# The FFN's gate and up projections made token-major, with an SBUF-to-SBUF step and block transposes

## What is computed

```python
h = rmsnorm_2(x, ffn_norm[l])
g = causal_dwconv(jnp.einsum('bsd,df->bsf', h, w_gate[l]), conv_w[l], conv_b[l])
u = jnp.einsum('bsd,df->bsf', h, w_up[l])
x = x + jnp.einsum('bsf,fd->bsd', jax.nn.silu(g) * u, w_down[l])
```

## Time and profile before

| | |
|---|---|
| median of 3 runs | 2015.3 us (2014.77 to 2015.37) |
| the profiled execution | 2015.61 us |
| its span, first to last instruction | 2013.7 us |
| mean granted TensorE clock | 0.999 |
| TensorE busy | 1996.9 us (99%) |
| VectorE busy | 1431.3 us (71%) |
| ScalarE busy | 1044.3 us (52%) |
| GpSimd busy | 404.8 us (20%) |
| DMA | 374.89 MB, 186 GB/s in the mean |

### The profile page before, as it was taken

How to read it: one execution, slowest core, us unless ns; L and a number is a source line. 1 busy time by engine, 2 the same in 40 slices (tenths; PEclk the granted TensorE clock), 3 DMA queues, 4 the chain that set the end, 5 groups by cost and what they waited for, 6 DMA issues and landing times.

```text
span 2013.7 us, 28421 instructions
## 1 busy us (share of the span) xinstructions
PE 1996.9 (99%) x11082; PEld 1734.2 (86%) x11082; DVE 1431.3 (71%) x2004; ACT 1044.3 (52%) x1575; POOL 404.8 (20%) x379
## 2 busy tenths in 40 slices
PE   8999999999999999999999999999999999999998
PEld 7888998888888888888888888888888888888886
DVE  6776788788788666876656679777775457777654
ACT  6654544466534654644555655455454345545444
POOL 0014544300000444430222335111010000101010
PEclk9999999999999999999999999999999999999999
DMA  9765666567655334665454446655666665656564
GB/s 331 232 190 149 194 186 198 188 212 242 221 171 171 120 121 133 191 203 196 154 170 147 147 163 189 203 187 182 188 195 191 197 189 189 191 187 197 190 195 150
DMA packets 103798, 374.89 MB, mean 186 GB/s; under 512 B 11728, under 2 KB 13168, under 8 KB 103152
## 3 DMA queue, kind: packets, MB, share of 16 engines
q1 hardware_dynamic: 103376, 372.54, 58.5%
q10 hardware_dynamic: 288, 0.52, 0.1%
HBM read 370.92 MB, written 2.10 MB: 185 GB/s over the span
## 4 chain that ended last, share of the span: by engine, by line
PE 95%; DVE 2%; DMA 2%; ACT 1%; issue 0%; SPq 0%; ACTq 0%
PE psg L574 42%; PE psg L575 22%; PE psg L641 3%; PE psg L643 2%; PE psg L642 2%; PE pst L669 2%; PE pss L669 2%; PE pst L671 2%; PE pss L670 2%; PE pst L670 2%; PE pss L671 2%; PE psg L615 1%; PE pst L615 1%; DMA s_stage<-in_mk 1%; DVE s_w L1827 1%; PE psg L618 1%
## 5 line engine op out<-in xcount | busy, mean ns | idle before, releaser
L1827 DVE TENSOR_TENSOR s_w<-s_stage,s_w 128x1024 fp32r<-128x1024 f32 (+2 forms) x690 | 856.7, 1243 | 384.6 <-ACT s_w L1204 383.4
L1204 ACT ACTIVATE s_w<-s_stage 128x1024 fp32r<-128x1024 f32 (+2 forms) x690 | 725.8, 1054 | 703.4 <-PE psg L575 471.2
L574 PE MATMUL psg<-s_ry,s_w 128*128 128x512 f32 x2560 | 896.5, 392 | 0.2 <-DVE s_w L1827 0.2
L575 PE MATMUL psg<-s_ry,s_w 128*128 128x256 f32 x2560 | 721.7, 282 | 0.0
L574 PEld LDWEIGHTS psg<-s_ry,s_w 128*128 128x128 f32 x2560 | 480.6, 188 | 103.5 <-issue 4.1
L575 PEld LDWEIGHTS psg<-s_ry,s_w 128*128 128x128 f32 x2560 | 484.3, 189 | 0.2
L574 PE MATMUL psg<-s_rh,s_w 128*128 128x512 f32 x1216 | 427.6, 394 | 0.3 <-DVE s_w L1827 0.3
L575 PE MATMUL psg<-s_rh,s_w 128*128 128x256 f32 x1216 | 342.8, 282 | 0.0
L574 PEld LDWEIGHTS psg<-s_rh,s_w 128*128 128x128 f32 x1216 | 228.3, 188 | 48.7 <-issue 1.0
L575 PEld LDWEIGHTS psg<-s_rh,s_w 128*128 128x128 f32 x1216 | 230.0, 189 | 0.6
L2758 POOL TENSOR_TENSOR s_hid<-s_hh,s_hid 128x256 fp32r<-128x256 f32 x44 | 53.6, 1218 | 563.3 <-ACT s_hid L1606 563.3
(11 more groups left out here) (420 smaller groups left out, 2464.1 us busy)
## 6 DMA issues: line engine op xcount, KB each, us to landing
s_stage<-in_wo SPq DMA_DIRECT2D x96, 512.0 KB, 3.7
s_stage<-in_wd SPq DMA_DIRECT2D x88, 512.0 KB, 4.2
s_stage<-in_wg SPq DMA_DIRECT2D x84, 512.0 KB, 3.9
s_stage<-in_wu SPq DMA_DIRECT2D x84, 512.0 KB, 3.9
s_stage<-in_ain SPq DMA_DIRECT2D x64, 512.0 KB, 3.9
s_stage<-in_wkv SPq DMA_DIRECT2D x32, 512.0 KB, 3.5
s_stage<-in_bq SPq DMA_DIRECT2D x24, 512.0 KB, 3.8
s_stage<-in_bzq SPq DMA_DIRECT2D x24, 512.0 KB, 3.5
```

The source lines that it names most:

```text
L574: e.matmul(o, M.WH[:, r, ws], xx, start=begin, stop=False)
L575: m = e.matmul(o[:, T:2 * T], M.WL[:, r, ws], xh, start=False, stop=end)
L1204: e.activation(M.weights(c, 0, n, shift), M.staged(c, n), ACT.Copy).then_inc(S["wh"], 1)
L1827: e.tensor_tensor(M.weights(c, 1, n, shift), M.staged(c, n), M.weights(c, 0, n, shift), ALU.subtract).then_inc(S["wl"], 1)
```

## The change

Gate and up are computed in 22 blocks of 8 units: block m is a token-major pair of 512 features, gate for even m and up for odd m. The first half gets 12 blocks (24 feature tiles), the second 10 (20 tiles); `down` takes 12 units for each 512 output columns in the first half and 10 in the second. The number of units stays 691.

A block's way to feature-major: ScalarE evacuates the two banks to `s_ev` with the token's norm factor (`evacuate`); SyncE issues 16 transfers of 32 partitions x 1 KB from `s_ev` to `s_sh` (`shift`), in program order after the load of the unit that stands 6 units past the block; VectorE transposes 32x32 blocks, one 128x256 instruction for each feature tile (`turn`), after waiting for all 16. The weights' columns are reordered on the host so that the blocks come out in order. From there convolution, silu, product and split run as before, now four tiles at a time; GpSimd's low parts stand in plain order. The norm gives two columns of token factors (`norm_cols`) instead of a row. In the second layer three semaphores are merged into one. The sums of column halves and the scalings by VectorE are gone.

```diff
+DOWN = (24, 20)
+BLOCKS = (range(12), range(12, 22))
@@ class Plan
+    def block(self, m):
+        tile = ("ff", m)
+        for t in range(2):
+            self.bank[tile, t] = ("sg"[m % 2], t)
+        for u in range(8):
+            self.unit(self.A[("wg", "wu")[m % 2]][8 * (m // 2) + u], 1024, SHIFT)
+            if u == 7:
+                self.half[tile] = len(self.half) + 1
+                self.close((tile, 0), "out_act")
+                self.close((tile, 1), "out_act")
+            self.step()
@@ TensorE
     for hv in range(2):
-        first = 22 * hv
-        if hv == 0:
-            group([(n, j) for j in range(2) for n in ("wg", "wu")], Y, ready("hf"), ffn_hook)
-            side.start(flips())
-            first = 2
-        for j in range(first, 22 * hv + 22):
-            tile(("wg", j), Y, ready("hf"))
-            tile(("wu", j), Y, ready("hf"))
+        for m in BLOCKS[hv]:
+            pair(("ff", m), Y, ready("hf"), ffn_hook if m == 0 else None)
+            if m == 0:
+                side.start(flips())
         down(hv)
@@ ScalarE
+    def evacuate(m):
+        w.wait_ge("nr_dve", 3 * NORM["ffn"] + 3)
+        if m:
+            w.wait_ge("shift", 256 * m)
+        for t in range(2):
+            if t:
+                w.wait_ge("units", P.end[("ff", m), 1])
+            else:
+                w.wait_ge("half", P.half["ff", m])
+            src = M.product(P.bank[("ff", m), t]).rearrange("p (r f) -> p r f", r=4)
+            e.activation(M.EV[:, :, t, :], src, ACT.Copy, scale=M.RC[0][:, t:t + 1]).then_inc(S["out_act"], 1)
+
+    def gate_block(m):
+        yield
+        yield
+        for c in range(5):
+            if c:
+                j = 2 * m + c - 1
+                w.wait_ge("ff_v", 2 * j + 2)
+                e.activation(M.CV[c - 1][:, :], M.CV[c - 1][:, :], ACT.Silu).then_inc(S["ff_s"], 1)
+            if c < 4:
+                j = 2 * m + c
+                w.wait_ge("turned", 4 * m + c + 1)
+                if m:
+                    w.wait_ge("ff_h", j - 3)
+                e.activation(M.CV[c][:, :], M.GG[c][:, :], ACT.Identity, scale=M.vec("cw2", j), bias=M.vec("cb", j)).then_inc(S["ff_c"], 1)
+            yield
+
+    def up_block(m):
+        hv = m // 12
+        for _ in range(3):
+            yield
+        for c in range(4):
+            j = 2 * m - 2 + c
+            w.wait_ge("ff_h", j + 1)
+            w.wait_ge("units", P.end["wd", 0, 3] if hv else P.end["wo2", KT - 1])
+            e.activation(M.HID[:, 0, j - DOWN[0] * hv, :], M.HH[j % 2][:, :], ACT.Copy).then_inc(S["hidh"], 1)
+            yield
@@
+        for m in BLOCKS[hv]:
             nxt(3)
+            if m == 0:
+                norm_cols("ffn", 0, 0)
+            nxt(4)
+            evacuate(m)
             nxt()
+            side.start(up_block(m) if m % 2 else gate_block(m))
@@ VectorE
+    def turn(m, c, dst):
+        w.wait_ge("shift", 256 * (m + 1))
+        e.transpose(dst.rearrange("p (t q i) -> p q t i", t=2, q=4), M.turned(c)).then_inc(S["turned"], 1)
+
+    def gate_block(m):
+        yield
+        for c in range(5):
+            if c:
+                j = 2 * m + c - 1
+                gg, cv = M.GG[c - 1], M.CV[c - 1]
+                w.wait_ge("ff_c", j + 1)
+                e.scalar_tensor_tensor(cv[:, 1:T], gg[:, 0:T - 1], M.vec("cw1", j), cv[:, 1:T], ALU.mult, ALU.add).then_inc(S["ff_v"], 1)
+                w.wait_ge("ff_v", 2 * j + 1)
+                e.scalar_tensor_tensor(cv[:, 2:T], gg[:, 0:T - 2], M.vec("cw0", j), cv[:, 2:T], ALU.mult, ALU.add).then_inc(S["ff_v"], 1)
+            if c < 4:
+                if m:
+                    w.wait_ge("ff_v", 2 * (2 * m + c) - 6)
+                turn(m, c, M.GG[c][:, :])
+            yield
+
+    def up_block(m):
+        yield
+        for c in range(5):
+            if c:
+                j = 2 * m - 2 + c - 1
+                w.wait_ge("ff_s", j + 1)
+                w.wait_ge("turned", 4 * m + c)
+                if j >= 2:
+                    w.wait_ge("hidl", j - 1)
+                e.tensor_tensor(M.HH[j % 2][:, :], M.UU[j % 2][:, :], M.CV[c - 1][:, :], ALU.mult).then_inc(S["ff_h"], 1)
+            if c < 4:
+                j = 2 * m - 2 + c
+                if j >= 2:
+                    w.wait_ge("ff_h", j - 1)
+                turn(m, c, M.UU[j % 2][:, :])
+            yield
@@
+        for m in BLOCKS[hv]:
             nxt(3)
+            if m == 0:
+                norm_cols("ffn", 0, 0)
+            nxt(5)
+            side.start(up_block(m) if m % 2 else gate_block(m))
         for n in range(4):
-            nxt(11)
+            nxt(DOWN[hv] // 2)
@@ SyncE
+    def shift(m):
+        w.wait_ge(*P.out[("ff", m), 1])
+        if m:
+            w.wait_ge("turned", 4 * m)
+        for r in range(4):
+            for q in range(4):
+                e.dma_start(M.SH[32 * r:32 * r + 32, q, :, :], M.EV[32 * q:32 * q + 32, r, :, :]).then_inc(S["shift"], 16)
@@
+    for m in range(22):
+        while issued[0] < P.end[("ff", m), 1] + 6:
+            weights()
+        shift(m)
     while issued[0] < NTOT:
         weights()
@@ layout
-    A["wg"] = b_pack(i["w_gate_2"][0], 8)
-    A["wu"] = b_pack(i["w_up_2"][0], 8)
+    for n, name in (("wg", "w_gate_2"), ("wu", "w_up_2")):
+        A[n] = v_pack(i[name][0].reshape(D, 11, 4, 4, 32).transpose(0, 1, 3, 2, 4).reshape(D, 5632))
```

More of the change, by code:

```diff
@@ L243, in residual @@
             self.tile((name, j), units(j))
+    def block(self, m):
[9 more added lines that the diff above has]
+            self.step()
     def down(self, hv):
         for n in range(4):
-            for u in range(11):
-                self.unit(self.A["wd"][44 * hv + 11 * n + u], 1024, SHIFT)
+            for u in range(DOWN[hv] // 2):
+                self.unit(self.A["wd"][2 * DOWN[0] * hv + DOWN[hv] // 2 * n + u], 1024, SHIFT)
                 self.step()
@@ L336, in plan @@
     for hv in range(2):
-        first = 22 * hv
-        if hv == 0:
-            P.group([(n, j) for j in range(2) for n in ("wg", "wu")], "gu")
-            first = 2
-        for j in range(first, 22 * hv + 22):
-            P.tile(("wg", j), P.halves("wg", j))
-            P.tile(("wu", j), P.halves("wu", j))
+        for m in BLOCKS[hv]:
+            P.block(m)
         P.down(hv)
@@ L622, in group, with pair @@
             unit()
-    def pair(t, x, ready):
+    def pair(t, x, ready, hook=None):
         banks = [P.bank[t, i] for i in range(2)]
@@ L646, in pair @@
             m.then_inc(S["units"], 1)
+            if hook is not None and u == 3:
+                hook()
             unit()
@@ L659, in down @@
     def down(hv):
-        x, there = both(M.HID), ready("hid", 22 * hv)
+        x, there, nk = both(M.HID), ready("hid", DOWN[0] * hv), DOWN[hv]
         def products(n, u, r, steps):
@@ L679, in down @@
                 held["st"[n % 2], t] = ("added", 2 * (4 * hv + n) + t + 1)
-            apart = 8 if hv and n == 3 else 11
+            apart = nk // 2 - (3 if hv and n == 3 else 0)
             for u in range(apart):
@@ L685, in down @@
             c = done[0]
-            for u in range(apart, 11):
+            for u in range(apart, nk // 2):
                 w.wait_ge("wl", c + u - apart + 1)
                 products(n, u, (c + u - apart) % NR, [(0, 0), (1, 0)])
-            for u in range(apart, 11):
+            for u in range(apart, nk // 2):
                 products(n, u, (c + u - apart) % NR, [(0, 1), (1, 1)]).then_inc(S["units"], 1)
@@ L1773, in scalar_program @@
     for hv in range(2):
-        first = 22 * hv
-        if hv == 0:
+        for m in BLOCKS[hv]:
             nxt(3)
[L1777 to L1784, removed]
+            if m == 0:
+                norm_cols("ffn", 0, 0)
+            nxt(4)
+            evacuate(m)
             nxt()
-            side.start(hidden(j))
-            nxt(3)
+            side.start(up_block(m) if m % 2 else gate_block(m))
+            if m == 0:
+                side.start(flips())
         for n in range(4):
-            nxt(11)
+            nxt(DOWN[hv] // 2)
             if hv and n == 0:
@@ L2751, in diff_head, with hidden @@
         put_y(YAT["diff"] + h, M.RH, h)
-    def hidden(j):
-        i = j % 22
-        for _ in range(5):
-            yield
+    def hidden(j, i):
         w.wait_ge("hidh", j + 1)
@@ L2858, in pool_program @@
     residual(post_f, early=12)
+    side.drain()
     for hv in range(2):
-        first = 22 * hv
-        if hv == 0:
-            ticks(6)
-            for j in range(2):
-                side.start(hidden(j))
-                tick()
-            first = 2
-        for j in range(first, 22 * hv + 22):
-            tick()
-            side.start(hidden(j))
-            ticks(3)
+        for i in range(DOWN[hv]):
+            hidden(DOWN[0] * hv + i, i)
         for n in range(4):
-            ticks(11)
             if hv and n < 3:
```

99 lines of the change are left out of this document (25 added, 74 removed).

## The result

The changed kernel takes 2105.6 us (median of 4 runs, 2102.89 to 2108.82); the kernel before, run beside it, took 2015.3. The ratio is 1.0449 [1.0436, 1.0461]: 90 us slower. The profiled execution took 2102.89 us, with a span of 2100.9 and a mean granted clock of 0.986 (0.999 before).

A forecast was written before the change was run, and what follows sets the result against it. TensorE, busy 99% of the span, was taken to bound the kernel. 2015.3 - 9.5 (faster matmul units) + 18.9 (22 waits of 0.86) = 2024.7 us; range 2005 to 2036 holding 0.85, the forecast's own 2019 to 2045.

The forecast's parts named there:

- TensorE's own gain: Gate and up stages: 482.6 us in place of 492.1, a gain of 9.5 us if TensorE never waits.
- The wait's place: Before a block's fifth unit, TensorE waits 0.86 us for VectorE's split; 22 times, 18.9 us.
- the time without waits: Whole kernel if TensorE never waits: 2005.8 us, from the median 2015.3 less 9.5.
- splits after the evacuation: ScalarE's split of unit E+2, E the block's last, ends 0.6 us later; low part at 3.2, needed at 5.44: hidden.
- the turn to down: Where the down projection starts, the last four hidden tiles are still on their way; this wait stays hidden.
- smaller norm: Two narrow norm matmuls in place of one, about 0.3 us; nothing on the path.
- The transpose: VectorE's block transpose: 0.34 us of queue time, upper end 0.64, which would add 6.6 us to the sum.
- The landing: Time for a transfer to land after its issue: 2.2 us, lower end 0.9, upper end 3.1.
- The issue: SyncE's 16 transfers a block: second issue 0.37 us after the first, then 0.475 each; ends 0.37 and 0.70.
- rival 3: Slower by more: descriptor queue fills up, issues pass 0.55 us; 2048, or about 2082 at 0.66. Chance 0.08.
- both ranges: Total time: 2005 to 2036 us, holding 0.85, and the forecast's own range, 2019 to 2045.
- Rival 1: Faster, no wait at blocks: issues of 0.37 us or a landing of 1.3, 2005.8 us. Chance 0.27.

The follow-up runs named there:

- eight transfers: Changed kernel with 8 transfers a block in place of 16, rows staying in their partitions, FFN data not the reference's: 2005.2 us, ratio 0.9948.
- two queues: Changed kernel with 10 of the 16 transfers issued by SyncE and six by ScalarE: 2006.7 us, ratio 0.9957.

## Why the prediction was right and wrong

**Right: the sign and its mechanism.** TensorE's own gain (482.6 forecast, 483.2 with eight transfers) and the time without waits (2005.8; 2005.2). The wait's place (the block's fifth unit, 22 times, two of them in down) and its chain, link by link. That all the rest hides: splits after the evacuation, the turn to down, the smaller norm. The transpose, 0.34 to the next instruction by forecast, took 0.37.

**Wrong: the size, by one term.** The failed step is "A transfer of 32 rows of 1 KB, the very size used here, also took 0.43 and let the next one start 0.48 later". It matched the rows by size and row count. But the sources of all those rows are DRAM tensors (`in_pos`, `in_lam`, `in_bt`, `in_con`), and the new transfers go from SBUF to SBUF, for which the trace of before had no row. The landing was given bounds for that reason. The issue, which stands in the sum 15 times where the landing stands once, had an upper end of 0.70, but I tied it to a full queue, in rival 3, and left it out of both ranges. The row at 24.26, to which that 0.48 runs, was itself longer: this issue, from DRAM too, took 0.55, and in the same timeline the next one starts 0.59 after it. No run shows why. In the order of the block ending at 1743.36:

| term | forecast | measured |
|---|---|---|
| boundary to first transfer | 0.89 | 0.92 (evacuation 0.69, not 0.60, begun 0.06 earlier) |
| first to 16th issue | 0.37 + 14 x 0.475 = 7.02 | 0.555 + 14 x 0.633 = 9.42 |
| landing of the last | 2.2 | 1.88 |
| transpose, split, start | 1.63 | 1.63 |
| TensorE starts | 11.74 | 13.85 |
| its wait (due at 10.88) | 0.86 | 2.97 |

The issues are 2.40 us late a block and the landing gives back 0.32. Over all 22 blocks the waits make 65.6 + 3.5 = 69.1 us in place of 18.9. The mean is 3.14 a block, somewhat above this one; in six blocks a single issue took 0.9 to 1.9 us. One end of a bound was misread as well: a store of 256 KB at 190 GB/s takes 1.4 us, not 1.3, so the landing's lower end is 0.8. Nothing hung on it.

**Wrong: nothing was forecast for the clock.** The rest, 26 to 27 us, is the stretches at half clock, and 2.4 the first distance after each wait. The sum mended: 2024.7 + 50.2 + 26.5 + 2.4 = 2103.8, against 2102.9 for the profiled execution (2105.6 for the median). The Trainium skill tells of it on its page "TensorE: Matmul & The Clock Gate", Part 1: an array that has been idle is clocked at half for a time. The trace agrees behind 16 of the 22 waits (0.427 us between matmuls after the wait, 0.227 before) and shows no such stretch behind the other six, of 2.9 to 3.0 us. A forecast that prices a wait of some microseconds should have asked for it.

**The rivals.** Rival 3 had the size for its upper end (0.66 us apart, wait 3.4, 2082; measured 0.633 and 3.0 to 3.1, with 2075 before the clock's part) but not the mechanism. The number outstanding doesn't set the spacing: with landings of 1.9 us some three transfers are outstanding at 0.633, and some four from DRAM at 0.464. I had tied that spacing to an unlikely cause and so gave it 0.08. Rival 1, no wait, is what the kernels with eight transfers and with two queues show. The sentence of the Trainium skill that stood beside it (page "DMA: Bandwidth & Descriptors", section "Issuing engines are not separate DMA queues": issuing from several engines saves only sequencer time, usually small) is no guide here: that sequencer time is 10.0 us for a train whose landing takes 1.9, and splitting it over two queues gained 99 us. The same page's fixed 2.0 us for a DMA, found for another issuing path, is close to the 1.8 measured.

## What to carry to other kernels

Count the DMA issues on a queue, and price one by a row with the same kind of source and destination, not only the same size; where no row has that kind, bound the issue as widely as the landing, since a train multiplies it. What a train costs depends on what stands behind it in program order: here moving six issues to another queue, or moving the waiting step two units later with the due loads put into the train, turned a kernel 4.5% slower than before into one 0.4% faster. And when a forecast has TensorE waiting for some microseconds many times, add the time after each wait at the lower clock.

## What the hardware showed that I had not expected

- In a train on SyncE an issue takes 0.59 to 0.60 us when both sides are in SBUF (0.633 to 0.643 apart), whether a transfer is 32 rows of 1 or 2 KB or 128 of 256 bytes, and 0.42 when 32 rows of 1 KB come from DRAM (0.464 apart). A load from DRAM right behind a train between SBUF and SBUF takes 0.58 too. ScalarE's queue issues beside SyncE's at nearly the same pace (median 0.61 us against 0.59).
- In the changed kernel, after 16 of 22 waits of 2.3 to 3.8 us the granted clock fell to half, beginning between 0.3 us before and 1.4 us after TensorE resumed, and cost 1.6 us each time.
- VectorE's product of 128x256 (line 2420, 2372 before) took 0.96 us in place of 0.42, and GpSimd's subtraction (2787) 1.53 in place of 1.20. In the timeline the product is long exactly where the subtraction runs beside it, and 0.41 to 0.42 elsewhere. The subtraction took 0.74 where VectorE was idle, 1.20 beside the end of a split, and 1.47 or more beside most of one, with or without the product. It cost no time here, and no run isolates it. Duration in ns, min/median/max:

```profile
L2420 DVE TENSOR_TENSOR s_hh<-s_uu,s_cv x44: 406/957/971, 1333.9 to 2000.9; 128x256 f32<-128x256 f32 x44
...
L2787 POOL TENSOR_TENSOR s_hid<-s_hh,s_hid x44: 738/1528/1542, 1334.8 to 2002.4; 128x256 fp32r<-128x256 f32 x44
```
